# The last eight row tiles of a down projection, taken by token range, with two norms in place of one

## The reference, cut to what matters

```
ffn = (silu(gate) * val) @ w_down        # 5632 -> 2048
x   = x + ffn
y   = x * rsqrt(mean(x * x, over the 2048 features) + 1e-6) * norm_final
```

## Time and profile before

| | |
|---|---|
| median of 3 runs | 1544.87 us (1544.74 to 1545.56) |
| the profiled execution, its own time | 1546.33 us |
| its span, first to last instruction | 1544.5 us |
| PE busy | 99% |
| granted TensorE clock | 0.999 |

### The profile page before, as it was taken

One profiled execution on the slowest core, in us unless ns is written; L12 is line 12 of the kernel. 1 busy time (PEld: TensorE's weight loads), 2 busy tenths in 40 slices (PEclk: granted clock), 3 DMA queues, 4 the chain that ended last, 5 costly groups with the idle time before them and its releaser, 6 DMA issues.

```text
span 1544.5 us, 33798 instructions
## 1 busy us (share of the span) xinstructions
PE 1531.0 (99%) x12498; PEld 1514.0 (98%) x12498; DVE 1022.7 (66%) x1475; ACT 661.1 (43%) x866; POOL 468.9 (30%) x581
## 2 busy tenths in 40 slices
PE   9999999999999999999999999999999999999998
PEld 8999999999999999999999999999999999999998
DVE  7655788888666666657676767777777764444443
ACT  6334345545566644444333333333333333333332
POOL 8993477877422201221111111111111100001100
PEclk9999999999999999999999999999999999999999
DMA  8877476676766586565555555454545465555552
GB/s 273 235 190 201 134 219 204 193 207 193 236 210 202 156 209 214 163 201 188 163 163 163 164 162 170 156 176 150 179 149 184 147 218 184 175 173 172 171 172 89
DMA packets 298990, 282.16 MB, mean 183 GB/s; under 512 B 35072, under 2 KB 290576, under 8 KB 298768
## 3 DMA queue, kind: packets, MB, share of 16 engines
q1 hardware_dynamic: 283008, 256.69, 54.7%
q10 hardware_dynamic: 13568, 16.62, 3.5%
q0 software_dynamic: 2320, 7.54, 1.5%
HBM read 266.73 MB, written 14.05 MB: 182 GB/s over the span
## 4 chain that ended last, share of the span: by engine, by line
PE 93%; POOL 5%; DMA 1%; issue 1%; ACT 0%; DVE 0%; POOLq 0%; ACTq 0%
PE banks L572 30%; PE banks L574 30%; PE banks L573 30%; POOL angle L1831 1%; POOL sm L1831 1%; POOL angle L1834 1%; PE banks L582 1%; POOL sm L1834 1%; PE banks L700 1%; PE banks L779 0%; PE banks L738 0%; PE banks L715 0%; DMA scratch_z<-zq 0%; POOL rdec L1834 0%; DMA params<-in_s_abs 0%
## 5 line engine op out<-in xcount | busy, mean ns | idle before, releaser
L1274 DVE TENSOR_TENSOR wlo<-raw,whi 128x1024 fp32r<-128x1024 f32 x443 | 557.8, 1273 | 285.7 <-ACT whi L917 281.3
L917 ACT ACTIVATE whi<-raw 128x1024 fp32r<-128x1024 f32 x443 | 462.2, 1052 | 538.8 <-PE banks L574 498.0
L573 PE MATMUL banks<-h_lo,whi 128*128 128x288 f32 x1408 | 415.7, 295 | 0.0
L574 PE MATMUL banks<-h_hi,wlo 128*128 128x288 f32 x1408 | 415.7, 295 | 0.0
L572 PE MATMUL banks<-h_hi,whi 128*128 128x288 f32 x1408 | 414.6, 294 | 0.0
L572 PE MATMUL banks<-hhi,whi 128*128 128x288 f32 (+1 forms) x912 | 271.3, 298 | 4.4 <-DVE hlo L1300 2.2
L574 PE MATMUL banks<-hhi,wlo 128*128 128x288 f32 (+1 forms) x912 | 269.0, 295 | 0.0
L573 PE MATMUL banks<-hlo,whi 128*128 128x288 f32 (+1 forms) x912 | 269.0, 295 | 0.0
L573 PEld LDWEIGHTS banks<-h_lo,whi 128*128 128x128 f32 x1408 | 264.6, 188 | 0.1
L574 PEld LDWEIGHTS banks<-h_hi,wlo 128*128 128x128 f32 x1408 | 264.4, 188 | 0.0
L572 PEld LDWEIGHTS banks<-h_hi,whi 128*128 128x128 f32 x1408 | 264.1, 188 | 0.1
(11 more groups left out here) (339 smaller groups left out, 2165.8 us busy)
## 6 DMA issues: line engine op xcount, KB each, us to landing
raw<-in_w_up SPq DMA_DIRECT2D x352, 256.0 KB, 3.3
raw<-in_w_in SPq DMA_DIRECT2D x223, 256.0 KB, 3.3
raw<-in_w_down SPq DMA_DIRECT2D x176, 256.0 KB, 3.0
raw<-in_w_glu SPq DMA_DIRECT2D x64, 256.0 KB, 3.2
raw<-in_w_out SPq DMA_DIRECT2D x64, 256.0 KB, 3.2
raw<-in_w_attn_proj SPq DMA_DIRECT2D x32, 256.0 KB, 3.9
scratch_gates<-gt ACTq DMA_DIRECT2D x16, 288.0 KB, 3.5
gbt<-scratch_gates POOLq DMA_DIRECT2D x8, 288.0 KB, 3.7
```

Of the source, the lines that this page charges most:

```text
L573: pe.matmul(out, h, xl[:, kt, :], start=False, stop=False)
L574: mm = pe.matmul(out, lo, xh[:, kt, :], start=False, stop=kt == nk - 1)
L917: act.activation(whi[:, s, :, 0:cols], raw[:, s, :, 0:cols], ACT.Copy).then_inc(hi_ready, 1)
L1274: dve.tensor_tensor(wlo[:, s, :, 0:cols], raw[:, s, :, 0:cols], whi[:, s, :, 0:cols], ALU.subtract).then_inc(lo_ready, 1)
```

## The change

In the last of the eight column groups, `group` now takes 36 of the 44 row tiles. The squares and sums follow the tokens:

- **The last eight row tiles** (two chunks) are run by a new function `last_tiles`, first for tokens 0 to 127 and both feature halves (banks `aux` 0 and 1), then for the other 160 tokens and both halves (`acc` 2 and 3). `by_feature` is gone.
- **DVE** adds the 36 row tiles' sum to `x3` in one piece, then the four parts as they come. It folds `sqacc` into the squares itself. The squares of the sample tokens are written four times beside each other (`by_copy`), so that PE sums them with one matmul in place of four.
- **PE's sums**: `sums_a` for tokens 0 to 127 is put after six of the eight row tiles of the first half of the 160; `sums_b` for the rest is run twice.
- **Two norms**: one inverse root for block 0, one for block 1 and the samples.
- **The output**: the nine tiles come as `Y_TILES` says, block 0 first; ACT scales tiles 0, 1, 3, 5, 6, DVE 2, 4, 7, 8. SP's six stores are grouped anew. The last `xg` pieces on ACT are 128 and 160 tokens wide.

```
-Y_TILES = ((0, 0), (0, 1), (0, 2), (1, 0), (1, 1), (1, 2), (0, 3), (2, 0), (1, 3))
+Y_TILES = ((0, 0), (0, 1), (0, 2), (0, 3), (1, 0), (1, 1), (2, 0), (1, 2), (1, 3))
+Y_ACT, Y_DVE = (0, 1, 3, 5, 6), (2, 4, 7, 8)
...
# SP
-            for t0, t1 in ((0, 1), (1, 3), (3, 5), (5, 6), (6, 7), (8, 9)):
+            for t0, t1 in ((0, 1), (1, 2), (2, 4), (4, 6), (7, 8), (8, 9)):
...
# PE
+            def last_tiles(out, cols, m, k0, k1):
+
+                for k in range(k0, k1):
+                    q, kt = k // KCH, KF - 2 * KCH + k
+                    pe.wait_ge(lo_ready, C_END + 87 + q)
+                    h, lo = (w[:, (C_END + 86 + q) % NSLOT, k % KCH, m * P:m * P + P] for w in (whi, wlo))
+                    pe.matmul(out, h, a_hi[:, kt, cols], start=k == 0, stop=False)
+                    pe.matmul(out, h, a_lo[:, kt, cols], start=False, stop=False)
+                    mm = pe.matmul(out, lo, a_hi[:, kt, cols], start=False, stop=k == 2 * KCH - 1)
+                return mm
+
+            def sums_a():
+
+                pe.wait_ge(sem("sq_last"), 1)
+                pe.matmul(aux[:, 3, 0:1], sq_last[:, 0, :], ones[:, 0:1], start=True, stop=True).then_inc(sem("sum_ready"), 1)
+
+            def sums_b(sq, first):
 
                 for b in range(2):
-                    pe.matmul(aux[:, 3 - b, 0:1], sq[:, b * P:b * P + P], ones[:, 0:1], start=first, stop=last)
-                for j in range(4):
-                    mm = pe.matmul(acc[TS * j:TS * (j + 1), 3, 0:1], sq[:, TP:T], ones[:, 0:1], start=first, stop=last)
+                    mm = pe.matmul(aux[:, 2 + b, 0:1], sq[:, b, :], ones[:, 0:1], start=first, stop=not first)
                 return mm
 
+            for m in range(2):
+                last_tiles(aux[:, m, 0:P], slice(0, P), m, 0, 2 * KCH).then_inc(sem("first_half"), 1)
+            pe.wait_ge(acc_free[1], 56)
+            last_tiles(acc[:, 2, 0:T - P], slice(P, T), 0, 0, 6)
+            sums_a()
+            last_tiles(acc[:, 2, 0:T - P], slice(P, T), 0, 6, 2 * KCH).then_inc(sem("first_half"), 1)
+            last_tiles(acc[:, 3, 0:T - P], slice(P, T), 1, 0, 2 * KCH).then_inc(sem("first_half"), 1)
...
             pe.wait_ge(sem("xg_ready"), 7)
-            pe.wait_ge(sem("sq_done"), 15)
-            pe.wait_ge(acc_free[1], 56)
-            sums(sqacc, True, False)
-            pe.wait_ge(sem("sq_last"), 1)
-            sums(sq_last[:, 0, :], False, False)
+            pe.wait_ge(sem("x3_last"), 3)
+            y_tile(0)
+            pe.wait_ge(sem("ms_ready"), 3)
             pe.wait_ge(sem("sq_last"), 2)
-            sums(sq_last[:, 1, :], False, True).then_inc(sem("sum_ready"), 1)
-            y_tile(0)
+            sums_b(sq_last[:, 2:4, :], True)
+            pe.wait_ge(sem("sq_last"), 3)
+            sums_b(sq_last[:, 4:6, :], False).then_inc(sem("sum_ready"), 1)
             y_tile(1)
             y_tile(2)
-            pe.wait_ge(sem("x3_last"), 2)
+            pe.wait_ge(sem("xg_ready"), 8)
             y_tile(3)
-            pe.wait_ge(sem("ms_ready"), 3)
+            pe.wait_ge(sem("x3_last"), 5)
             y_tile(4)
             y_tile(5)
-            pe.wait_ge(sem("xg_ready"), 8)
+            pe.wait_ge(sem("yo_ready1"), 1)
+            pe.wait_ge(sem("xg_ready"), 9)
             y_tile(6)
+            pe.wait_ge(sem("yo_ready1"), 2)
             y_tile(7)
             pe.wait_ge(sem("yo_ready0"), 1)
             y_tile(8)
...
# ACT
+            last_scaled(0, slice(0, P), 2)
+            last_scaled(1, slice(0, P), 3).then_inc(sem("xg_ready"), 1)
+            act.wait_ge(sem("ms_ready"), 3)
+            act.activation(rtok[:, 4:5], rtok[:, 0:1], ACT.Sqrt).then_inc(sem("root_ready"), 1)
+            last_scaled(0, slice(P, T), 4)
+            act.wait_ge(sem("rtok_ready"), 1)
+            y_evac(0)
+            act.wait_ge(sem("ms_ready"), 4)
+            act.activation(rtok[:, 5:7], rtok[:, 1:3], ACT.Sqrt).then_inc(sem("root_ready"), 1)
+            y_evac(1)
+            last_scaled(1, slice(P, T), 5).then_inc(sem("xg_ready"), 1)
+            y_evac(3)
+            act.wait_ge(sem("rtok_ready"), 2)
+            y_evac(5)
+            y_evac(6)
...
# DVE, for tokens 128 to 287 (the part for tokens 0 to 127 is alike, with its mean and inverse root ahead of this)
+            for m in range(2):
+                x = last_rows(m, slice(P, T), acc[:, 2 + m, 0:T - P], m + 4)
+                sq = sq_last[:, 2 + 2 * m:4 + 2 * m, :]
+                samples = lambda a: bc(a, 1, 4)
+                by_copy = sq[:, 1, :].rearrange("p (j t) -> p j t", j=4)
+                ins = dve.tensor_tensor(sq[:, 0, :], x[:, 0:P], x[:, 0:P], ALU.mult)
+                if m == 0:
+                    own(ins)
+                ins = dve.tensor_tensor(by_copy, samples(x[:, P:T - P]), samples(x[:, P:T - P]), ALU.mult)
+                if m == 0:
+                    own.link(ins)
+                    dve.tensor_tensor(sq[:, 0, :], sq[:, 0, :], sqacc[:, P:TP], ALU.add)
+                    ins = dve.tensor_tensor(by_copy, by_copy, samples(sqacc[:, TP:T]), ALU.add)
+                ins.then_inc(sem("sq_last"), 1)
```

More of the change, by code:

```diff
@@ L858, in _ @@
                 for g in range(4):
-                    group((g + 1) % 2, 52 + 2 * half + (g + 1) // 2, C_END + 44 * half + 11 * g, KF, a_hi, a_lo, slot0=11 * g % 4,
-                          before={10: (lambda: pe.wait_ge(sem("a_ready"), N_UP),)} if half + g == 0 else {}, by_feature=half + g == 4)
-            def sums(sq, first, last):
+                    group((g + 1) % 2, 52 + 2 * half + (g + 1) // 2, C_END + 44 * half + 11 * g, KF if half + g < 4 else KF - 2 * KCH, a_hi, a_lo, slot0=11 * g % 4,
+                          before={10: (lambda: pe.wait_ge(sem("a_ready"), N_UP),)} if half + g == 0 else {})
@@ L1242, in _ @@
                         act.wait_ge(acc_free[(g + 1) % 2], 53 + k // 2 + k % 2)
[L1243 to L1249, removed]
@@ L1250, in _, with last_scaled @@
-            act.wait_ge(sem("rtok_ready"), 1)
-            for t in range(1, 9, 2):
+                        for m in range(2):
+                            ins = act.activation(xg[:, 2 * k + m, :], x3[:, 2 * k + m, :], ACT.Copy, scale=nvec[:, 32 + 2 * k + m:33 + 2 * k + m])
+                        ins.then_inc(sem("xg_ready"), 1)
+            def last_scaled(m, cols, x_added):
+                act.wait_ge(sem("x3_last"), x_added)
+                return act.activation(xg[:, 14 + m, cols], x3[:, 14 + m, cols], ACT.Copy, scale=nvec[:, 46 + m:47 + m])
@@ L1774, in _ @@
                     else:
[L1775 to L1783, removed]
@@ L1785, in _, with last_rows @@
-            dve.wait_ge(sem("sum_ready"), 2)
-            for b, total in enumerate((aux[:, 3, 0:1], aux[:, 2, 0:1], acc[:, 3, 0:1])):
-                ins = dve.tensor_scalar(rtok[:, b:b + 1], total, 1.0 / D, EPS, ALU.mult, ALU.add)
+                        dve.wait_ge(chunks_used, c + 9)
+                        dve.tensor_tensor(x3[:, 14:16, :], acc[:, 0:2, 0:T], x3[:, 14:16, :], ALU.add).then_inc(sem("x3_last"), 1)
+            def last_rows(m, cols, bank, done):
+                dve.wait_ge(sem("first_half"), done - 1)
+                dve.wait_ge(sem("x3_last"), done - 1)
+                x = x3[:, 14 + m, cols]
+                dve.tensor_tensor(x, bank, x, ALU.add).then_inc(sem("x3_last"), 1)
+                dve.wait_ge(sem("x3_last"), done)
+                return x
@@ new lines, in _ @@
+            dve.wait_ge(sem("cst_saved"), 2 * N_UP + 1)
+            dve.wait_ge(sem("sq_done"), 15)
+            for m in range(2):
+                x = last_rows(m, slice(0, P), aux[:, m, 0:P], m + 2)
+                own.link(dve.tensor_tensor(sq_last[:, m, :], x, x, ALU.mult))
+                if m == 0:
+                    own.link(dve.tensor_tensor(sq_last[:, 0, :], sq_last[:, 0, :], sqacc[:, 0:P], ALU.add))
+                else:
+                    dve.tensor_tensor(sq_last[:, 0, :], sq_last[:, 0, :], sq_last[:, 1, :], ALU.add).then_inc(sem("sq_last"), 1)
@@ new lines, in _ @@
+            dve.wait_ge(sem("sum_ready"), 2)
+            dve.tensor_scalar(rtok[:, 0:1], aux[:, 3, 0:1], 1.0 / D, EPS, ALU.mult, ALU.add).then_inc(sem("ms_ready"), 1)
+            inverse_root(rtok[:, 0:1], rtok[:, 4:5], nw[0][:, 0:1], lambda: dve.wait_ge(sem("root_ready"), 3))
+            dve.tensor_tensor(rtok[:, 4:5], rtok[:, 4:5], nw[0][:, 0:1], ALU.mult).then_inc(sem("rtok_ready"), 1)
+            for m in range(2):
+                x = last_rows(m, slice(P, T), acc[:, 2 + m, 0:T - P], m + 4)
[6 more added lines that the diff above has]
+                ins = dve.tensor_tensor(by_copy, samples(x[:, P:T - P]), samples(x[:, P:T - P]), ALU.mult)
+                if m == 0:
+                    own.link(ins)
+                    dve.tensor_tensor(sq[:, 0, :], sq[:, 0, :], sqacc[:, P:TP], ALU.add)
+                    ins = dve.tensor_tensor(by_copy, by_copy, samples(sqacc[:, TP:T]), ALU.add)
+                ins.then_inc(sem("sq_last"), 1)
@@ L1788, in _ @@
```

(11 more changed lines are left out.)

24 lines of the change are left out of this document (12 added, 12 removed).

## The result

The changed kernel took 1549.43 us in the median of 14 runs, the kernel before 1546.17 us in the median of 14 runs beside them. The ratio is 1.0019, 95% interval 1.0012 to 1.0026: slower by 1.9 to 4.0 us. Applied to the 1544.87 us on which the forecast was made it gives 1547.8 us; the forecast was 1548.2.

The account below looks back on a forecast made before the run. PE, busy 99% of the span, was taken to bound the kernel until a last chain waiting on the stores' DMA engines. Last start +5.2 us and tail -1.94 gave +3.3, so 1548.2 us against the median, range 1546.0 to 1561.0.

Parts of the forecast that it names:

- The stream: Last eight row tiles' matmuls on PE: 96 short ones at 118 ns in place of 48, +4.95 us, plus 0.24 for sums_a.
- The cover: Second part's matmuls on PE: sums_a waits for nothing, and DVE's first norm fits beside the 3.5 us of matmuls after it.
- The tail: From the last product matmul's start to the end: 11.84 us against 13.78, so -1.94 us (-0.6 to -3.2).
- The landing: End of the tail: 1.5 us pass from the end of the stores' draining to the end.
- The rival that the early tile brings nothing: Tail: stores' end hangs on the last scaled tile, gain only 0.6, total +4.6 us, 1549.5 us; no chance of its own.
- The sum: Whole kernel: last start +5.2 us, tail gives back 1.94, together +3.3 us; chance of slower by over 0.2% 0.60.
- The columns rival: Split stream: columns set the short matmuls' pace, stream only +0.9, total -0.5 us, 1544.4 us; chance 0.09.
- The fallback to more passes: Split stream: short f32r matmuls drop to plain f32's rate, stream +15.7, total +14.0 us, 1558.9 us; chance 0.25.
- the columns case: Split stream if columns set the pace: about 69 ns for 128 columns and some 82 for 160; chance 0.09.

Follow-up runs that it names:

- e3: Changed kernel with the 96 split matmuls loading only 64 of 128 weight columns; stream 6.56 us, tail 12.72 us, one run.
- e6: Changed kernel with SP storing the four tiles of block 0 in one DMA in place of three; stream 10.79 us, tail 13.77 us, one run.
- e2: Changed kernel with both passes over the last eight row tiles streaming 224 columns in place of 128 and 160; stream 10.82 us, tail 12.17 us, one run.
- e4: Changed kernel with only the last four row tiles taken by token range and sums_a between the 160 tokens' feature halves; ratio to kernel before 1.0020, tail 16.28 us.
- e5: Kernel before with its undivided stream, but the changed kernel's order of the end and two norms; ratio to kernel before 1.0005, tail 14.93 us.
- e9: The kernel before run again, nothing changed; stream 6.25 us, tail 13.90 us, one run.
- e8: The changed kernel run again, nothing changed; stream 10.80 us, tail 11.98 us, one run.

## Why the prediction was right

**The stream.** The forecast took 118 ns for both widths from the sums' one-column matmuls; it was 112, and equal at both. That is nearer to the distance between their weight loads (110 ns) than between their matmuls (118). The growth was +4.55 us with `sums_a`, forecast +5.2. The term was 0.65 us too large, 0.58 of it the pace and 0.07 `sums_a`. The Trainium skill's sustained 81 ns for 128 columns ("TensorE: Matmul & The Clock Gate", "Back-to-back issue gap") does not hold for this kernel's f32r loads, at 111 ns.

**The cover.** `sums_a` waited for nothing, DVE finished the first norm at 1535.87, 1.75 us ahead of the last start, went through the adds and squares of the second part's first feature half, and then stood idle 0.77 us before the last add. e3 shows the price when the stream is quick: 0.6 us where 0.3 was forecast.

**The tail.** Step by step after the last start: first issue at 1.53 us (forecast 1.56), second inverse root 3.31 (3.4), last scaling 7.12 (7.2), end of draining 10.2 (10.3). The landing of the last store then took 1.9 us in place of 1.5. So the tail gave 1.70, forecast 1.94; the step that was off is the landing, which the forecast took from the kernel before. The rival that the early tile brings nothing fell by e6.

**The sum** was +3.3 us, the pieces gave +2.85, and the runs +1.9 to +4.0. Two misses of opposite sign stand behind the close sum, 0.65 us too much for the stream and 0.24 us too much for the gain, so part of the closeness is luck. The forecast stood just on the slower side of 0.2%, with 0.60 for it; the measured 0.19% (0.12 to 0.26) stands at that line and does not decide it.

**The rivals.** The columns rival (1544.4 us) fell: e2 moved 56% more columns for nothing. Its own price was also too high. Where the loads are short, the split costs little: in e3 the stream took 6.56 us against 6.25, and 0.2 of that is `sums_a`. The fallback to more passes, to which I gave 0.25 and the upper 10 us of the range, fell too: at 60 ns for 128 columns a short f32r matmul runs at the same rate per column as a long one. The Trainium skill, "FP8 and Floating Point Precision", section "TensorE Precision Notes", gives four passes for true FP32 and a truncated read for its reduced form. It names no width, and e3's pace agrees with that. The range was wide for a case that the trace had merely not shown.

## What to carry to other kernels

In these runs an f32r matmul whose weights change every time costs the larger of its columns and its weight load. A load of 128 columns is worth about 244 moving columns (112 ns / 0.46), so cutting 288 columns in two adds 91 ns a matmul (2 x 112 - 133). That was measured for 128 and 160 columns, and no less for twice 224; it should hold for any cut that leaves both parts under some 244. Before splitting a stream to start its tail early, multiply that by the matmuls split, and compare it with what the tail can give: here 48 x 91 ns against 1.75 us. With the 0.17 us of `sums_a` paid, the break-even lay near 17 matmuls, an estimate, if the first norm still found its cover. With 24 matmuls split, in e4, it no longer did. In a tail that ends in stores, look at when the DMA engines begin to drain and whether the next tiles keep them busy from there (e5), and not at when the last tile is ready.

## What was not expected of the hardware

**The clock of the tail.** In e4 PE was busy 0.24 and 0.37 of two windows of 1 us, and then its granted clock fell: 0.6 of 2.4 GHz in the mean of the window from 1535, and 0.5 (1.2 GHz) in each one after it until 1542. In the changed kernel PE had one wait of 0.16 us in the tail and in e5 one of 0.60, and both ran their transposes at the full clock. In this execution the 20 transposes took 2.13 us more at the lower clock, which is more than the wait of 1.39 us itself. That the wait brought the fall is inferred from this order of events; no experiment varied it.

**The pace with half loads.** 60 ns at 128 columns was below what I took for the floor of the columns case (69 ns), since I had added the fixed part of the 288-column matmul. Between 128 and 288 columns it is 0.45 to 0.46 ns a column with almost nothing fixed.

**The unchanged part.** The last eight row tiles started at 1524.47 and 1522.65 us in the two profiled runs of the kernel before (before and e9), and at 1526.82 and 1523.82 in those of the changed one. Windows of 100 us have PE idle in the first 500 us alone: 6.8 us in before and 9.0 in the first run of the changed kernel. PE's waits for DVE there add up to 5.1 and 7.3 us, so they are 2.2 of the 2.35 us between these two. e9 and e8 had 3.2 and 4.7 us idle, but started only 1.82 and 0.65 us earlier than before, so the idle time is not all of it, and the rest stays open. The scatter is as large as the effect that was measured, and only the pieces of the profile, or many runs, part them.
